# A two-block network on one Trainium2 core: Hyena transforms issued two jobs ahead, output weights loaded in two halves, and five extra products at the end of each output stage

## The reference, cut to what matters

```python
def bidir_long_conv(u, h_fwd, h_bwd, bias):
    n = u.shape[1]
    lag0 = h_fwd[:1] + h_bwd[:1]
    k = jnp.concatenate([lag0, h_fwd[1:], jnp.zeros((1, C_WIDTH), jnp.float32), h_bwd[:0:-1]], axis=0)
    uf = jnp.fft.rfft(u.astype(jnp.float32), n=2 * n, axis=1)
    kf = jnp.fft.rfft(k, axis=0)
    y = jnp.fft.irfft(uf * kf[None], n=2 * n, axis=1)[:, :n]
    return (y + u.astype(jnp.float32) * bias.astype(jnp.float32)).astype(u.dtype)

# in hyena_mixer, for x and for ctx
        z = v
        for o in range(C_ORDER):
            z = gx[o] * bidir_long_conv(z, filt[:, 0, o], filt[:, 1, o], filt_bias[o])
        return (z * jax.nn.silu(gate)) @ w_out

# in second_block, behind each mixer
        x = x + gate_x * rmsnorm(yx, g_post[layer])
        if with_ctx_out:
            ctx = ctx + gate_c * rmsnorm(yc, g_post[layer])
```

## Time and profile before

| what | value |
|---|---|
| median of 3 runs | 3219.52 us (3218.55 to 3222.61) |
| the profiled execution, its own time | 3221.93 us |
| its span | 3220.2 us |
| TensorE busy in the span | 2993.0 us, 93% |
| VectorE busy in the span | 1046.4 us, 32% |
| granted TensorE clock, mean | 0.97 of full speed |
| first transform of the conv stage starts at | 2499.12 us |
| its output stage's first product starts at | 2714.87 us |

### The profile page before, as it was taken

One profiled execution on the slowest core, in us unless ns is written; L12 is line 12 of the kernel. 1 busy time (PEld: TensorE's weight loads), 2 busy tenths in 40 slices (PEclk: granted clock), 3 DMA queues, 4 the chain that ended last, 5 costly groups with the idle time before them and its releaser, 6 DMA issues. The chain is left out here.

```text
span 3220.2 us, 34707 instructions
## 1 busy us (share of the span) xinstructions
PE 2993.0 (93%) x13879; PEld 1790.7 (56%) x13879; DVE 1046.4 (32%) x2203; ACT 751.1 (23%) x1698; POOL 156.1 (5%) x256
## 2 busy tenths in 40 slices
PE   6999997999899879999999999999999686999999
PEld 3447755555454466567645666545556344474674
DVE  3442352322212121025431027433330774210242
ACT  2111461000000032134331138520001110321441
POOL 0000000110111000000000002101110000000000
PEclk9999997999999979999999999999999888999999
DMA  6665434999999921120101220012241324022200
GB/s 228 233 230 200 161 124 155 381 385 388 389 389 387 357 99 53 36 82 1 40 0 39 67 92 2 14 41 90 88 170 62 107 76 144 1 59 56 76 1 33
DMA packets 242838, 445.59 MB, mean 138 GB/s; under 512 B 26799, under 2 KB 108927, under 8 KB 239356
## 3 DMA queue, kind: packets, MB, share of 16 engines
q1 hardware_dynamic: 230678, 407.15, 35.8%
q0 software_dynamic: 9488, 22.11, 2.0%
q10 hardware_dynamic: 2518, 14.16, 1.1%
HBM read 413.20 MB, written 37.78 MB: 140 GB/s over the span
## 5 line engine op out<-in xcount | busy, mean ns | idle before, releaser
L378 PE MATMUL hyena_in_main<-hT,weight_slots 128*128 128x256 f32 (+1 forms) x1024 | 333.1, 488 | 5.0 <-PEq L1395 5.0
L378 PEld LDWEIGHTS hyena_in_main<-hT,weight_slots 128*128 128x128 f32 x1024 | 195.3, 191 | 141.9 <-issue 128.8
L2651 PE MATMUL moe_ph<-expert_weights,moe_x_T 128*64 128x256 f32 x2048 | 239.5, 387 | 20.4 <-DMA expert_weights<-w 11.2
L2651 PEld LDWEIGHTS moe_ph<-expert_weights,moe_x_T 128*64 128x64 f32 x2048 | 147.5, 139 | 128.0 <-issue 44.5
L378 PE MATMUL swa_in_main<-hT,weight_slots 128*128 128x512 f32 (+1 forms) x576 | 190.3, 490 | 5.0 <-PEq L1395 5.0
L1418 PE MATMUL post_y<-expert_weights,hT 128*128 128x512 f32 x384 | 169.1, 600 | 15.4 <-DMA expert_weights<-c_w_out 14.2
L1615 PE MATMUL qkv_main<-hT,weight_slots 128*128 128x512 f32 (+1 forms) x384 | 167.8, 580 | 0.9 <-PEq L1058 0.9
L378 PE MATMUL mla_down_main<-hT,weight_slots 128*128 128x512 f32 (+1 forms) x448 | 160.9, 516 | 0.9 <-DVE expert_weights L492 0.9
L378 PEld LDWEIGHTS swa_in_main<-hT,weight_slots 128*128 128x128 f32 x576 | 110.2, 192 | 84.6 <-issue 77.5
L378 PE MATMUL mla_up_main<-expert_weights,weight_slots 128*128 128x512 f32 (+1 forms) x416 | 146.5, 511 | 3.7 <-PEq L329 3.3
L1418 PE MATMUL post_y<-expert_weights 128*128 128x512 f32 x320 | 138.5, 593 | 1.6 <-PEq L840 1.6
(11 more groups left out here) (408 smaller groups left out, 4061.9 us busy)
## 6 DMA issues: line engine op xcount, KB each, us to landing
expert_weights<-w SPq DMA_DIRECT2D x96, 2048.0 KB, 22.4
first_w_out<-w_mod SPq DMA_DIRECT2D x12, 2048.0 KB, 8.4
expert_weights<-w_mod SPq DMA_DIRECT2D x12, 2048.0 KB
weight_slots<-w_in SPq DMA_DIRECT2D x16, 1024.0 KB
weight_slots<-c_w_in SPq DMA_DIRECT2D x16, 1024.0 KB
weight_slots<-a_w_in SPq DMA_DIRECT2D x14, 1024.0 KB
expert_weights<-scr_spectra SPq DMA_DIRECT2D x12, 1024.0 KB, 4.9
weight_slots<-b_w_in SPq DMA_DIRECT2D x10, 1024.0 KB
```

What stands on the lines that cost most here:

```text
L378: mm = pe.matmul(main[u][0:unit.rows, 0:unit.cols], lhsT, rhs, start=(c == 0), stop=(c == r.kc - 1))
L2651: mm = pe.matmul(bank[half * T:(half + 1) * T, 0:HF], x_T[:, c, :], w[:, c, half * HF:(half + 1) * HF], start=(c == 0), stop=(c == KD - 1))
```

## The change

It has three parts. (1) `steps` now issues the turns two jobs ahead. SyncE issues the gates of a back step's successor one job later in its list, in `gates_behind`. (2) The output weights are loaded in two halves of 2 MB: the first half while job 4 is worked on, the second at the end of SyncE's list, behind the last gates. To free the room of the first half, `K` moves into `left` and a new tile, the four-kind product is made in `U` itself in place of `prod` and therefore behind the two cross products, and two of the four `g1` buffers move into `rest`. (3) Each output stage with a layer behind it ends, on TensorE, with five products of 128x128 with 128x512 whose result nobody reads.

```diff
@@ project_out, TensorE
+def unread_products(pe, bank, lhsT, rhs, n):
+    for _ in range(n):
+        pe.matmul(bank, lhsT, rhs, start=True, stop=True)
...
                     if normed is not None and k:
                         normed.turn_on_tensor(pe, k - 1)
+                if normed is not None:
+                    pe.wait_ge(s_added, n - 2)
+                    unread_products(pe, y[n % 3][:, 0:BANK], z_T[:, 0, 0:P], w_sb[:, 0, 0:BANK], 5)
@@ long_conv
-    steps = [("turn", 0, k) for k in range(SEGS["x"][2])]
-    for j in range(len(jobs)):
-        if j + 1 < len(jobs):
-            steps += [("turn", j + 1, k) for k in range(SEGS[jobs[j + 1][2]][2])]
-        steps.append(("back", j))
+    steps = []
+    for j in range(-2, len(jobs)):
+        if j + 2 < len(jobs):
+            steps += [("turn", j + 2, k) for k in range(SEGS[jobs[j + 2][2]][2])]
+        if j >= 0:
+            steps.append(("back", j))
...
-        K, parts = [room[:, b] for b in range(2)], [room[:, 2 + b] for b in range(2)]
-        U, prod = (left[:, k * KINDS * HALF:(k + 1) * KINDS * HALF].rearrange("p (k n) -> p k n", k=KINDS) for k in range(2))
+        U, K0 = (left[:, k * KINDS * HALF:(k + 1) * KINDS * HALF].rearrange("p (k n) -> p k n", k=KINDS) for k in range(2))
+        K, parts = [K0, st.sb("spectrum1", [P, KINDS, HALF])], [room[:, 2 + b] for b in range(2)]
...
-        g1, gate = [st.sb(f"g1_{b}", [P, X])[:] for b in range(4)], [flat[1][:, b * X:(b + 1) * X] for b in range(4)]
+        g1 = [rest[:, b * X:(b + 1) * X] for b in range(2)] + [st.sb(f"g1_{b}", [P, X])[:] for b in range(2)]
+        gate = [flat[1][:, b * X:(b + 1) * X] for b in range(4)]
@@ long_conv, SyncE
+                def gates_behind(j):
+                    for m in range(4 if jobs[j][0] else 0):
+                        n = nth_result[j, m]
+                        if n + 4 < len(results):
+                            sp.wait_ge(s_read, banks.upto(first["back", j] + m))
+                            gates_in(n + 4)
...
+                halves = [slice(0, KD // 2), slice(KD // 2, KD)]
                 for step in steps:
                     if step[0] == "turn":
                         spectrum_in(nth[step])
-                    else:
-                        if step == ("back", len(jobs) - 1):
-                            sp.wait_ge(s_Y, 2 * len(turns))
-                            load_out_weights(sp, consts["w_out"], w_out)
-                        for m in range(4 if jobs[step[1]][0] else 0):
-                            n = nth_result[step[1], m]
-                            if n + 4 < len(results):
-                                sp.wait_ge(s_read, banks.upto(first[step] + m))
-                                gates_in(n + 4)
+                    elif step[1]:
+                        gates_behind(step[1] - 1)
+                        if step[1] == len(jobs) // 2:
+                            load_out_weights(sp, consts["w_out"][:, halves[0], :], w_out[0:D // 2, :])
+                sp.wait_ge(s_step, 4 * (len(turns) - 1) + 2)
+                load_out_weights(sp, consts["w_out"][:, halves[1], :], w_out[D // 2:D, :])
@@ long_conv, VectorE, one turn
                     if t:
-                        dve.wait_ge(s_prod, 3 * t)
+                        dve.wait_ge(s_Y, 2 * t)
                     tt(U[:, 0:2, :], f[:, 0:KINDS:2, :], f[:, 1:KINDS:2, :], ALU.add).then_inc(s_step, 1)
                     tt(U[:, 2:4, :], f[:, 0:KINDS:2, :], f[:, 1:KINDS:2, :], ALU.subtract).then_inc(s_step, 1)
                     dve.wait_ge(s_K[t % 2], 16 * (t // 2 + 1))
                     dve.wait_ge(s_step, 4 * t + 2)
-                    if t:
-                        dve.wait_ge(s_Y, 2 * t)
-                    tt(prod[:], U[:], k, ALU.mult).then_inc(s_prod, 1)
                     tt(cross[0][:], U[:, 1:KINDS:2, :], k[:, 0:KINDS:2, :], ALU.mult).then_inc(s_prod, 1)
                     tt(cross[1][:], U[:, 0:KINDS:2, :], k[:, 1:KINDS:2, :], ALU.mult).then_inc(s_prod, 1)
-                    dve.wait_ge(s_prod, 3 * t + 1)
-                    tt(prod[:, 0:KINDS:2, :], prod[:, 0:KINDS:2, :], prod[:, 1:KINDS:2, :], ALU.add).then_inc(s_step, 1)
+                    dve.wait_ge(s_prod, 3 * t + 2)
+                    tt(U[:], U[:], k, ALU.mult).then_inc(s_prod, 1)
                     dve.wait_ge(s_prod, 3 * t + 3)
+                    tt(U[:, 0:KINDS:2, :], U[:, 0:KINDS:2, :], U[:, 1:KINDS:2, :], ALU.add).then_inc(s_step, 1)
                     dve.wait_ge(s_step, 4 * t + 3)
-                    tt(prod[:, 1:KINDS:2, :], cross[0][:], cross[1][:], ALU.subtract).then_inc(s_step, 1)
+                    tt(U[:, 1:KINDS:2, :], cross[0][:], cross[1][:], ALU.subtract).then_inc(s_step, 1)
                     dve.wait_ge(s_step, 4 * t + 4)
                     if step[1] >= 2:
                         dve.wait_ge(s_mm, last_out(step[1] - 2) + 1)
-                    tt(y[:, 0:KINDS:2, :], prod[:, 0:2, :], prod[:, 2:4, :], ALU.add).then_inc(s_Y, 1)
-                    tt(y[:, 1:KINDS:2, :], prod[:, 0:2, :], prod[:, 2:4, :], ALU.subtract).then_inc(s_Y, 1)
+                    tt(y[:, 0:KINDS:2, :], U[:, 0:2, :], U[:, 2:4, :], ALU.add).then_inc(s_Y, 1)
+                    tt(y[:, 1:KINDS:2, :], U[:, 0:2, :], U[:, 2:4, :], ALU.subtract).then_inc(s_Y, 1)
```

More of the change, by code:

```diff
@@ L212, in load_out_weights @@
 def load_out_weights(sp, tile, w):
-    sp.dma_start(tile[:], rows(w)).then_inc(Stage.out_in, 16)
+    sp.dma_start(tile, rows(w)).then_inc(Stage.out_in, 16)
     Stage.out_loaded += 16
@@ L610, in _ @@
                         sp.wait_ge(s_max, w_out_after + 1)
-                    load_out_weights(sp, consts["w_out"], w_out)
+                    load_out_weights(sp, consts["w_out"][:], w_out)
             @block.tensor
@@ L3436, in copies, with long_conv @@
                  self.bank[k % 2][:, 0:TOK].rearrange("p (t n) -> p t n", n=P)).then_inc(self.s_out[which], 1)
-def long_conv(nc, a, v, g0, tables, spectra, scr, w_out, left, consts):
+def long_conv(nc, a, v, g0, tables, spectra, scr, w_out, left, rest, consts):
     jobs = [(order, half, seg) for order in range(2) for half in range(2) for seg in ("x", "ctx")]
-    steps = [("turn", 0, k) for k in range(SEGS["x"][2])]
-    for j in range(len(jobs)):
-        if j + 1 < len(jobs):
-            steps += [("turn", j + 1, k) for k in range(SEGS[jobs[j + 1][2]][2])]
-        steps.append(("back", j))
+    steps = []
[4 more added lines that the diff above has]
+            steps.append(("back", j))
     def outputs(step):
@@ L3503, in spectrum_in @@
                         sp.wait_ge(s_prod, 3 * (t - 1))
-                    sp.dma_start(K[t % 2], spectra[t]).then_inc(s_K[t % 2], 16)
+                    sp.dma_start(K[t % 2][:], spectra[t]).then_inc(s_K[t % 2], 16)
                 def gates_in(n):
@@ L3598, in multiply @@
                     _, _, seg = jobs[step[1]]
-                    f, k = parts[t % 2], K[t % 2]
+                    f, k = parts[t % 2], K[t % 2][:]
                     y = Y[seg, step[2]]
@@ L3683, in hyena @@
               for name in ("cos", "sin", "icos", "isin") for seg, (_, _, nb) in SEGS.items()}
-    left = room.tile(2 * KINDS * HALF)
+    left, rest = room.tile(2 * KINDS * HALF), room.tile(D)
     v = hT[:].rearrange("p c n -> p (c n)").rearrange("p (t n) -> p t n", n=D)
@@ L3687, in hyena @@
     places = [spare[:, k * TOK:(k + 1) * TOK] for k in range(KD * D // TOK)]
-    places += [left[:, k * TOK:(k + 1) * TOK] for k in range(left.shape[1] // TOK)] + [room.tile(TOK)]
+    places += [left[:, k * TOK:(k + 1) * TOK] for k in range(left.shape[1] // TOK)] + [rest[:, 0:TOK]]
     hyena_in(nc, a, hT, scr, taps, consts,
@@ L3692, in hyena @@
     consts["z_T"] = hT
-    long_conv(nc, a, v, g0, tables, spectra, scr, a["c_w_out"][0], left, consts)
+    long_conv(nc, a, v, g0, tables, spectra, scr, a["c_w_out"][0], left, rest, consts)
 def first_range(a, layer):
```

1 line of the change is left out of this document (removed).

## The result

| | before | after |
|---|---|---|
| median | 3219.52 us (5 runs, 3218.16 to 3222.61) | 3202.76 us (5 runs, 3199.76 to 3203.38) |
| ratio | | 0.9946, 95% interval 0.9935 to 0.9957 |
| span of the profiled execution | 3220.2 us | 3201.1 us |
| granted clock, mean | 0.971 | 0.975 |
| conv stage, first transform to the output stage's first product | 215.75 us | 204.68 us |

What follows compares the result with a forecast made beforehand. TensorE, busy 93% of the span, was taken as the bound, with time to win only where it idles or runs at half clock. Conv 10.2 plus products 8.3 gave 18.5 us off 3219.5: 3201.0 us, range 3196 to 3210.

Steps and rivals of the forecast that it cites:

- Added waits: VectorE's conv turns: each added wait costs 0.18 us, two within a turn (12.13 us), a third where turns adjoin (12.31).
- The walk: Conv stage's middle: start times followed turn by turn over VectorE and TensorE, with 48.6 us for two jobs.
- The stall for `Y` in T4.0: VectorE, inside job 4's first turn: it waits 8 us, from 2596, for the buffer that TensorE's back step reads.
- the order two ahead only enters its period earlier: Conv stage: issuing turns two jobs ahead doesn't shorten the two-job period, 48.6 us against 47 in before.
- The tail: Conv stage's end: the 7.82 us spectrum stall goes, weights' second half issued at 2695.8, output stage starts at 2704.6.
- Its landing: DMA of the output weights' second half: 2 MB land 8.8 us after issue, with gates still under way.
- Conv part: Conv stage: the output stage starts at 2704.6 instead of 2714.87, a gain of 10.2 us.
- The five products: TensorE at three stage changes: unread products keep the clock up, saving cold starts of 2.5, 2.6 and 3.2, sum 8.3 us.
- The cover of the products: End of the output stage: the products end at 2808.75, VectorE's last copy at 2808.97, 0.2 us to spare.
- Both together: Conv gain 10.2 and products 8.3 sum to 18.5 us, giving 3201.0 us; chance 0.70.

Runs made afterwards that it cites:

- e3: Changed kernel with the turns one job ahead as before, all else kept: 3206.31 us, conv stage 207.46 us.
- e5: Changed kernel with the list of steps reordered, an x job's back step between the two turns of the x job two ahead: 3185.81 us.
- e2: Kernel before with the five unread products as its only change: 3214.69 us, 0.9981 of before.
- e1: Changed kernel without the five unread products at the end of the output stages: 3209.96 us, 0.9966 of before.
- e9: Changed kernel with seven unread products instead of five: 3205.67 us, 0.9958 of before.
- e6: Changed kernel with the output weights loaded whole, 4 MB, where their second half stands: 3206.14 us, conv stage 207.90 us.
- e4: Changed kernel with the output weights' second half issued ahead of job 6's gates instead of behind job 7's: 3199.03 us, 0.9929 of before.
- e5b: Changed kernel with the reordered list of steps and the weights' second half issued ahead of job 7's gates: 3180.42 us, 0.9880 of before.
- e7: Changed kernel with two unread products instead of five: 3205.78 us, 0.9957 of before.
- e8: The changed kernel itself, timed again: 3202.22 us, 0.9947 of before.

## Why the prediction was right

3201.0 us was forecast, within 3196 to 3210; 3202.76 was measured. To compare the steps, 4.5 us are added to the times of the changed kernel's trace, since its conv stage starts that much earlier.

- *Added waits, 0.18 us each.* Half right. The one ahead of a turn costs 0.19, the two inside 0.12 to 0.13. A turn took 12.17 us, not 12.31. The Trainium skill ("VectorE: DVE Perf Modes", "The DRAIN you can't avoid") reports eight copies that took the same time with a semaphore behind each as with one behind the last. That doesn't carry over to these instructions: three added waits lengthened a turn by 0.40 us.
- *The walk.* G0 forecast at 2569.9, measured 2569.6; T4.1 at 2606.4, measured 2606.2; G2 at 2618.5, measured 2618.2; G4 at 2667.1, measured 2666.4; T7 at 2669.8, measured 2669.1. The stall for `Y` in T4.0: about 8, measured 8.87. One step of the walk was off and cost little: the clock fell 0.3 us behind the stage's first product, for 3.4 us, so that VectorE's first turn began 1.7 us late; it then ran beside less of GpSimd's work, and the second turn was 0.3 us late. The claim that the order two ahead only enters its period earlier and doesn't shorten it is shown by the rows, 48.2 us from B2 to B4 against 47.3 in before, and by e3, which lacks that order and loses only 2.8 us. e5, with the same work in another order and without the stall, has 40.7.
- *The tail.* T7 took 13.7 us and not 13.1, since GpSimd's factors lengthened four of its instructions (one row above shows 1.75 for 1.22). G5 at 2682.9, measured 2682.8. First gates of job 6 at 2683.4, measured 2683.3. The weights' second half at 2695.8, measured 2695.8. Its landing: 8.8 us forecast, 7.96 measured, so the 2 MB row alone (8.4) would have been the better price. Output stage at 2704.6, measured 2703.8. Conv part 10.2 us forecast, 11.07 measured.
- *The five products.* 8.3 us forecast. In the traces the first records of the three stages are 2.35, 2.48 and 2.99 us shorter, 7.8 together; by the medians e2 gives 6.2 and e1 against the changed kernel 5.8. What a cold start costs isn't the same in each execution: mla_down's first 32 records took 10.13 us in before and 8.53 in e1, behind the same pause. In before's trace the clock stayed at half for 6.8 us at each of the three changes, in e1's for 3.4, 6.8 and 3.4. The forecast took the profiled execution's three prices, and that execution was 2.4 us above the median. That is the mis-sized term: the products are worth about 6 us in the median, not 8.3.
- *The cover of the products.* "0.2 us to spare": e9 shows that two more cost 1.43 us each time, and four more records take 1.7, so about 0.3 us was left.
- *Both together.* 18.5 us forecast, 16.8 measured; the conv part came out 0.9 larger and the products about 2 smaller. That the two errors partly cancel is luck.

What the prediction summed into one figure and the runs took apart: three quarters of the conv gain don't come from the order two ahead. One job ahead with everything else kept wins 8.3 of the 11.1 us. Nearly all of these 8.3 lie behind the issue of the weights (7.4 by the rows of e3), where a load of 2 MB lands in 8.0 us instead of 15.3. Not all of the 7.4 is the size of the load: undoing it alone, in the order two ahead, cost 3.2 (e6, of it 5.1 more for the landing, less 1.9 for the sooner issue). The gates' place and the longer turns were not undone by themselves, so what each is worth is read from rows only.

## What to carry to other kernels

Issuing a producer's work further ahead moves a pause and doesn't remove it, where a ring of buffers and a single-buffered result tie the two engines the other way round: walk one whole period, and place the consumer's step where its buffers are waited for (e5: 16.7 us more for a reordered list). Read a DMA queue's list at its end: a large load whose room has been free for long shouldn't stand behind small ones that wait for something else (e4, e5b: 4 to 5 us). An engine that waits out a change of stage can be kept warm by work nobody reads, but only as much as its cover: measure one less and one more.

## What the runs showed of the hardware

The clock's fall doesn't keep to the pause. All places here are read in windows of 0.1 us. Behind the pauses of 5.04 us in before it fell 3.0, 3.2 and 4.3 us after TensorE had stopped. With pauses of 3.32 us (e7) it fell once within the pause and twice 0.5 and 1.4 us after work had begun again, so a pause that shows full speed from end to end isn't therefore free. Ahead of the conv stage, behind a pause of 1.32 us, it fell in three of the twelve traces (the changed kernel, e4, e5b), 0.3 us behind the first product: the stage's first 72 records took 32.84 us in the changed kernel and 31.14 in e8. Behind the pauses of 0.74 and 0.45 us at the changes of stage no trace has a fall. The half-clock stretches at all these places lasted 3.4 or 6.8 us.

VectorE's additions and products of 1024 columns ran 1.6 to 1.8 us instead of 1.22 beside a GpSimd product of 256 columns, and up to 2.3 beside one of 512 columns (e3). There the two took turns at paying: at 2674.2 VectorE's product took 2.30 us and GpSimd's its usual 1.27, at 2676.5 VectorE's took 1.21 and GpSimd's 2.33. Two of GpSimd's own products of 256 columns beside VectorE took 3.23 us in the changed kernel, and the next two 4.44, where two such products later in the stage took 1.41.
